# Stick-breaking running sums: one fp32 summand and two matmuls, against a high and a low fp32r part and four matmuls

## The chip, the cores and the metric

The kernel runs on one core of a Trainium2 chip. The metric is device time in microseconds of one execution. The kernel before takes 1051.0 us (median of 3 runs, 1050.75 to 1051.4).

## What is computed

The program is a two-layer encoder trunk on 256 tokens of width 1024: in each layer a SwiGLU block, a mixer, a second SwiGLU block and a gated embedding. The mixer of layer 0 has 8 forgetting-attention heads and 8 stick-breaking heads. The change touches the stick-breaking heads alone:

```python
def stick_breaking_attention(q, k, v):        # 8 heads, 256 tokens, head width 64
    z = einsum('bhqd,bhkd->bhqk', qi, k) * scale
    strict = kpos[None, :] < qpos[:, None]
    log_1m = where(strict, log_sigmoid(-z), 0.0)
    incl = cumsum(log_1m, axis=3, reverse=True)          # running sum over keys
    excl = concatenate([incl[..., 1:], 0], axis=-1)
    a = where(strict, exp(log_sigmoid(z) + excl), 0.0)
    return einsum('bhqk,bhkd->bhqd', a, v)
```

## The kernel before

Five engines run their own instruction lists and meet at semaphores. The order on each engine is written out by hand. Weights stream from HBM in chunks of 256 columns through a ring of four buffers (`raw`). ScalarE writes the high fp32r part of each half chunk (L585), VectorE the low part (L879), and TensorE multiplies three times (high by high, high by low, low by high). In the mixer such a product of 128 by 256 is L1292 to L1294, and for the value tiles L1485 to L1487.

The attention heads are laid as steps between these products. There are 16 heads in layer 0: steps 0 to 7 are forgetting attention, steps 8 to 15 the stick-breaking heads, which this text numbers 0 to 7. Up to head 2 one product tile of 24 matmuls stands between steps (`mixer_in`); from then on half tiles of 12 (`mixer_out`), two of them between an odd head's sums and those of the next even head.

Scores are kept with keys on the partitions, in a PSUM bank of 384 columns: keys 0 to 127 by all 256 queries, then keys 128 to 255 by queries 128 to 255. For a stick-breaking pair the steps are:

- TensorE, `stick_pair` (L1547, L1550, L1552): mask and scores of both heads.
- VectorE, `stick_abs` (L1123): absolute value into `probs`. For the odd head it waits (`buffers_free`) until the running sums of the odd head before it are done, since they read `probs`.
- ScalarE: exp (L773) and ln(1 + ...) (L775), in place.
- VectorE, `stick_sp` (L1129): max(score, 0) plus that logarithm, written over `probs`. This is the summand.
- TensorE, `middle` (L1589, L1590): a triangular matrix of minus ones times the summand is added onto the 384 columns of scores in PSUM, and a full matrix of minus ones times the last 128 columns onto the middle 128. Both are plain fp32.
- ScalarE (L767): exp of the bank into `probsT`. Then TensorE's `values_pair` (L1611, L1615), two steps later.

On VectorE an even step is: abs of the even head, low part of an older output (L1118), abs of the odd head, one L879, summand of the even head. An odd step is the summand of the odd head and one L879 if one is due. In `mixer_out` the residual addition L1158 stands between steps. On TensorE the sums of an odd head stand right behind `stick_pair` of the next pair, and those of an even head right behind a product tile (or two half tiles).

Of the kernel before, what the change touches and what calls it, by code (L numbers as in the profile page):

```python
# [5 lines left out]
ALU = mybir.AluOpType  # L6
ACT = mybir.ActivationFunctionType
AX_X = mybir.AxisListType.X
F32 = mybir.dt.float32
# [142 lines left out]
def trunk(nc, x, p, ln_ffn1, w_ffn1_gu, w_ffn1_down, ln_mix, w_in_even, b_forget, w_out_even, w_in_odd,  # L152
# [14 lines left out]
    with ExitStack() as ctx:  # L167
# [15 lines left out]
        with ExitStack() as region:  # L183
            osp = region.enter_context(nc.sbuf_tensor("osp", [P, KD, 2, SEQ], F32R))
            qT = region.enter_context(nc.sbuf_tensor("qT", [P, 8, SEQ], F32))
            kT = region.enter_context(nc.sbuf_tensor("kT", [P, 8, SEQ], F32))
            vN = region.enter_context(nc.sbuf_tensor("vN", [P, TOK, 2 * GROUP_W], F32))
        with ExitStack() as region:
            hankel = region.enter_context(nc.sbuf_tensor("hankel", [P, HEADS, 257], F32))
        with ExitStack() as region:  # L190
            xin = region.enter_context(nc.sbuf_tensor("xin", [P, TOK, D_MODEL], F32))
            gin = region.enter_context(nc.sbuf_tensor("gin", [P, P], F32))
            proj = region.enter_context(nc.sbuf_tensor("proj", [P, KD, SEQ], F32))
            yT = region.enter_context(nc.sbuf_tensor("yT", [P, KD, SEQ], F32))
            yN = region.enter_context(nc.sbuf_tensor("yN", [P, TOK, D_MODEL], F32))
            rel_sb = region.enter_context(nc.sbuf_tensor("rel_sb", [HEADS, 3 * P], F32))
        hff = sb("hff", [P, KF, 2, SEQ], F32R)


# [8 lines left out]
        bias = sb("bias", [P, HEADS, LOGITS], F32)  # L208
        probs = sb("probs", [P, 2, LOGITS + 2], F32)
        probsT = sb("probsT", [P, 4, LOGITS], F32)  # L210

        swa_scale = sb("swa_scale", [P, HEADS // 2], F32)
        mask_causal = sb("mask_causal", [P, LOGITS], F32)
# [19 lines left out]
        nhalf = sb("nhalf", [P, 2], F32)  # L233
        rcol = sb("rcol", [P, 2], F32)
        rtmp = sb("rtmp", [P, 2], F32)
        row_sq = sb("row_sq", [P, len(GATE_ROWS)], F32)
        rfin = sb("rfin", [P, TOK], F32)
        bf = sb("bf", [P, HEADS], F32)
        nsink = sb("nsink", [P, HEADS], F32)
        fl = sb("fl", [P, TOK, HEADS], F32)  # L240
        fa = sb("fa", [P, TOK, HEADS], F32)
        logf = sb("logf", [P, TOK, HEADS], F32)
        fcum = sb("fcum", [P, TOK, HEADS], F32)
        negmax = sb("negmax", [P, 2, 2], F32)
# [34 lines left out]
        k_swapped = sem("k_swapped")  # L279
        scores_done, logits_ready = sem("scores_done"), sem("logits_ready")  # L280
        exp_done, pt_done, pt_ready = sem("exp_done"), sem("pt_done"), sem("pt_ready")
        sb_abs, sb_e, sb_log, sb_sp, incl_done, sb_a = sem("sb_abs"), sem("sb_e"), sem("sb_log"), sem("sb_sp"), sem("incl_done"), sem("sb_a")
        norm_step, probs_ready, pv_done = sem("norm_step"), sem("probs_ready"), sem("pv_done")
        os_hi, os_lo = sem("os_hi"), sem("os_lo")
# [286 lines left out]
        def _(act):  # L571
# [124 lines left out]
            def mixer_in(ph, norm):  # L696
                if ph.layer == 1:
                    act.wait_ge(tile_done, state["T"])
                    src = bass.AP(rel_scratch, 0, [[1, P], [3 * P, HEADS], [1, 257]])
                    act.dma_start(hankel[:], src).then_inc(rel_back, 16)  # L700
                for n, (chunk, col, what, idx, scale) in enumerate(IN_TILES[ph.layer]):
                    next_tile()
                    if is_v(what):

                        if what == "v":
                            group, j, t = idx
                            start, w = GROUP_W * group + 256 * j, 256
                        else:
                            t, start, w = idx, GROUP_W, P
                        act.wait_ge(rcol_ready, norm + 1)  # L710
                        act.activation(vN[:, t, start:start + w], ps[:, in_bank(n), 0:w], ACT.Copy,
                                       scale=rcol[:, t:t + 1]).then_inc(v_ready, 1)
                    if not slots(ph.layer, n):
                        advance(in_units(ph, n))
                    if ph.layer == 1 and (what, idx) == ("vd", 0):

                        act.wait_ge(*written(1, n - 1))
                        act.dma_start(kT[0:HD, 5, :], kT[HD:P, 4, :]).then_inc(k_swapped, 16)
                        act.dma_start(kT[HD:P, 5, :], kT[0:HD, 4, :]).then_inc(k_swapped, 16)
                    if ph.layer == 1 and n == 3:  # L720
                        act.wait_ge(rel_back, 16)
                        for col, far in ((0, P), (P, 2 * P), (2 * P, P)):
                            act.activation(bias[:, :, col:col + P], hankel[:, :, far:far - P:-1], ACT.Copy,
                                           scale=-1.0).then_inc(chunk_bias, 1)
                    if ph.layer == 0 and n == FORGET_TILE + 1:

                        nc.scalar.preload_act_table_set("natural_log_exp_and_others")
                        act.wait_ge(f_step, 2)
                        act.activation(fa[:], fa[:], ACT.Exp, scale=-1.0).then_inc(f_act, 1)
                        act.wait_ge(f_act, 1)  # L730
                        act.activation(fa[:], fa[:], ACT.Ln, bias=1.0).then_inc(f_act, 1)
                    for i in slots(ph.layer, n):
                        attention_step(ph.layer, i)
                        advance(in_units(ph, n))
# [135 lines left out]
        def _(dve):  # L870
# [236 lines left out]
            def attention_step(layer, i, units):  # L1107


                first, n = 2 * HEADS * layer, 2 * HEADS  # L1110
                if layer == 1 and i == 0:
                    dve.wait_ge(chunk_mask, 2)
                g = first + i
                def low_of_values():
                    if 4 <= i and i % 2 == 0:
                        pair = (g - 4) // 2
                        dve.wait_ge(os_hi, pair + 1)
                        dve.tensor_tensor(osp[:, pair % KD, 1, :], ps[:, BANK_O[pair % 2], 0:SEQ], osp[:, pair % KD, 0, :].bitcast(F32),  # L1118
                                          ALU.subtract).then_inc(os_lo, 1)

                def stick_abs(e):
                    buffers_free(e)
                    dve.tensor_scalar(probs[:, e % 2, 0:LOGITS].bitcast(I32), ps[:, stick_bank(e), 0:LOGITS].bitcast(I32), NO_SIGN, None,  # L1123
                                      ALU.bitwise_and).then_inc(sb_abs, 1)

                def stick_sp(e):
                    row = probs[:, e % 2, 0:LOGITS]
                    dve.wait_ge(sb_log, stick_no[e] + 1)
                    dve.scalar_tensor_tensor(row, ps[:, stick_bank(e), 0:LOGITS], 0.0, row, ALU.max, ALU.add).then_inc(sb_sp, 1)  # L1129

                if i < n and is_sb[g] and i % 2 == 0:
                    stick_abs(g)
                    low_of_values()
                    stick_abs(g + 1)
                    advance(units)
                    stick_sp(g)
                elif i < n and is_sb[g]:
                    stick_sp(g)
                    advance(units)
                elif i < n and i % 2 == 0:  # L1140
                    logits(g)
                    low_of_values()
                    logits(g + 1)
                    advance(units)
                    normalise(g)
                elif i < n:
                    normalise(g)
                    advance(units)
                else:
                    low_of_values()  # L1150
                    advance(units)
# [126 lines left out]
        def _(pe):  # L1278
# [296 lines left out]
            def middle(g):  # L1575
                s = g % 2
                if not is_sb[g]:

                    pe.wait_ge(probs_ready, soft_no[g] + 1)
                    if soft_no[g]:  # L1580
                        pe.wait_ge(pt_ready, soft_no[g])
                    for b in range(3):
                        mm = pe.transpose(ps[:, BANK_PT, b * P:(b + 1) * P], probs[:, s, prob_block(b)], ident[:])  # L1583
                    mm.then_inc(pt_done, 1)
                else:

                    S, sp_ = ps[:, stick_bank(g)], probs[:, s]
                    pe.wait_ge(sb_sp, stick_no[g] + 1)
                    pe.matmul(S[:, 0:LOGITS], negtri[:], sp_[:, 0:LOGITS], start=False, stop=True, skip_group_check=True)  # L1589
                    pe.matmul(S[:, P:SEQ], negones[:], sp_[:, SEQ:LOGITS], start=False, stop=True,  # L1590
                              skip_group_check=True).then_inc(incl_done, 1)

            def values_pair(g):
# [210 lines left out]
```

## Time and profile before

| | |
|---|---|
| median of 3 runs | 1051.0 us |
| the profiled execution | 1051.11 us |
| its span | 1049.4 us |
| TensorE busy | 1034.7 us (99%) |
| VectorE busy | 757.6 us (72%) |
| ScalarE busy | 587.7 us (56%) |
| granted TensorE clock, mean | 0.997 of full speed |

The span runs from the first to the last instruction of the trace; 1.7 us of the execution lie around it. Busy times add up instructions. Matmul records overlap (a matmul of 256 columns is recorded as 0.28 us, and the next one begins 0.12 us after it), so for TensorE the distance between starts is what a matmul costs the stream.

### The profile page before, as it was taken

What the parts mean: (1) busy time and instruction counts of PE and PEld (TensorE: products, weight loads), DVE (VectorE), ACT (ScalarE), POOL (GpSimd) and SP (SyncE); (2) the same over time, 40 slices, a digit from 0 to 9 for tenths busy, and PEclk for the clock granted to TensorE, in tenths of its full rate; (3) what the DMA queues carried; (4) which work ended last, traced back from release to release, by engine and by line L of the source; (5) the groups of instructions that cost most, each with busy time, mean ns of one, the idle gap of its engine ahead of it and who ended that gap; (6) DMA issues with size and microseconds to landing.
All of it is one profiled execution on the core that took longest, in us unless ns stands there. A gap on an engine that the chain in (4) does not pass through costs nothing.

```text
span 1049.4 us, 18321 instructions
## 1 busy us (share of the span) xinstructions
PE 1034.7 (99%) x6624; PEld 926.4 (88%) x6624; DVE 757.6 (72%) x1352; ACT 587.7 (56%) x1002; POOL 52.0 (5%) x100
## 2 busy tenths in 40 slices
PE   9999999999999999999999999999999999999996
PEld 8888888999888888888998888889987888888896
DVE  5988765677558888666788778656766787786576
ACT  6666545445646566554566565445665665654463
POOL 1000001000002000000010000000000200000000
PEclk9999999999999999999999999999999999999998
DMA  9675457573324655456747664477733375645741
GB/s 317 212 232 165 143 159 214 174 240 113 121 91 156 220 185 186 138 163 202 231 129 239 197 197 133 144 207 237 242 97 111 118 240 197 197 134 145 205 158 41
DMA packets 225223, 184.46 MB, mean 176 GB/s; under 512 B 3640, under 2 KB 223504, under 8 KB 225168
## 3 DMA queue, kind: packets, MB, share of 16 engines
q1 hardware_dynamic: 222832, 180.94, 55.1%
q10 hardware_dynamic: 2336, 2.81, 0.9%
q8 instruction: 32, 0.52, 0.2%
q14 instruction: 23, 0.19, 0.1%
HBM read 182.54 MB, written 1.06 MB: 175 GB/s over the span
## 4 chain that ended last, share of the span: by engine, by line
PE 93%; DVE 3%; issue 1%; DMA 1%; ACT 1%; SPq 0%; DVEq 0%; ACTq 0%
PE ps L1370 42%; PE ps L1375 22%; PE ps L1292 4%; PE ps L1301 4%; PE ps L1293 4%; PE ps L1294 4%; PE ps L1485 2%; PE ps L1302 2%; PE ps L1486 2%; PE ps L1487 2%; DVE wsp L879 1%; PE ps L1570 1%; DMA raw<-in_w_ffn_gu_dram 1%; PE ps L1611 1%; PE ps L1583 1%
## 5 line engine op out<-in xcount | busy, mean ns | idle before, releaser
L879 DVE TENSOR_TENSOR wsp<-raw,wsp 128x1024 fp32r<-128x1024 f32 (+1 forms) x381 | 416.1, 1108 | 61.0 <-ACT wsp L585 60.2
L585 ACT ACTIVATE wsp<-raw 128x1024 fp32r<-128x1024 f32 (+1 forms) x381 | 354.5, 957 | 26.4 <-PE ps L1294 21.5
L1370 PE MATMUL ps<-xsA,wsp 128*128 128x512 f32 x960 | 229.0, 391 | 0.0
L1370 PEld LDWEIGHTS ps<-xsA,wsp 128*128 128x128 f32 x960 | 176.4, 188 | 34.3
L1370 PE MATMUL ps<-hff,wsp 128*128 128x512 f32 x616 | 145.0, 390 | 0.0
L1370 PEld LDWEIGHTS ps<-hff,wsp 128*128 128x128 f32 x616 | 113.8, 188 | 22.7
L1375 PEld LDWEIGHTS ps<-xsA,wsp 128*128 128x128 f32 x960 | 123.0, 191 | 4.5
L1375 PE MATMUL ps<-xsA,wsp 128*128 128x256 f32 x960 | 124.7, 283 | 0.0
L894 DVE TENSOR_TENSOR sq<-ps,sq 128x512 f32<-128x512 f32 x88 | 60.5, 687 | 87.6 <-ACT sq L601 87.2
L601 ACT ACTIVATE sq<-ps 128x512 f32<-128x512 f32 x88 | 51.9, 590 | 111.0 <-PE ps L1375 109.3
L647 ACT ACTIVATE xsA<-xT,gains 128x256 fp32r<-128x256 f32 x48 | 24.4, 507 | 135.2 <-DVE xT L1028 120.4
L1292 PE MATMUL ps<-xsA,wsp 128*128 128x256 f32 x296 | 85.7, 289 | 0.4 <-DVE wsp L879 0.4
L1293 PE MATMUL ps<-xsA,wsp 128*128 128x256 f32 x296 | 83.7, 283 | 0.0
L1294 PE MATMUL ps<-xsA,wsp 128*128 128x256 f32 x296 | 83.6, 283 | 0.0
L1370 PE MATMUL ps<-xsB,wsp 128*128 128x512 f32 x336 | 80.2, 391 | 0.0
L1375 PEld LDWEIGHTS ps<-hff,wsp 128*128 128x128 f32 x616 | 77.6, 191 | 2.2
L604 ACT ACTIVATE silu<-gate_n 128x256 f32<-128x256 f32 x88 | 37.0, 420 | 75.1 <-DVE gate_n L896 75.1
L1375 PE MATMUL ps<-hff,wsp 128*128 128x256 f32 x616 | 78.3, 283 | 0.0
L1370 PEld LDWEIGHTS ps<-xsB,wsp 128*128 128x128 f32 x336 | 61.7, 188 | 12.0
L896 DVE TENSOR_TENSOR gate_n<-sq,rstd 128x512 f32<-128x512 f32 x88 | 60.9, 692 | 3.0
L1292 PEld LDWEIGHTS ps<-xsA,wsp 128*128 128x128 f32 x296 | 56.7, 191 | 1.0 <-DVE wsp L879 0.6
L1293 PEld LDWEIGHTS ps<-xsA,wsp 128*128 128x128 f32 x296 | 56.7, 192 | 0.1
(204 smaller groups left out, 1452.6 us busy)
## 6 DMA issues: line engine op xcount, KB each, us to landing
raw<-in_w_ffn_gu_dram SPq DMA_DIRECT2D x87, 1024.0 KB, 5.1
raw<-in_w_ffn_down_dram SPq DMA_DIRECT2D x64, 704.0 KB, 4.7
raw<-in_w_in_even_dram SPq DMA_DIRECT2D x11, 1024.0 KB, 6.0
raw<-in_w_in_odd_dram SPq DMA_DIRECT2D x9, 1024.0 KB, 6.1
raw<-in_w_ple_gate_dram SPq DMA_DIRECT2D x8, 1024.0 KB, 6.2
raw<-in_w_out_even_dram SPq DMA_DIRECT2D x4, 1024.0 KB, 5.6
raw<-in_w_out_odd_dram SPq DMA_DIRECT2D x4, 1024.0 KB, 6.2
raw<-in_w_ple_proj_dram SPq DMA_DIRECT2D x2, 1024.0 KB, 5.1
```

Source lines behind the costliest of these rows:

```text
L585: act.activation(wsp[:, s, 0, half * n:(half + 1) * n], raw[:, s, half * n:(half + 1) * n], ACT.Copy).then_inc(hi, 1)
L601: act.activation(cross[:], ps[:, b:b + 3:2, SEQ:], ACT.Copy).then_inc(gu_cross, 1)
L604: act.activation(silu[:], gate_n[:, 0], ACT.Silu).then_inc(gu_silu, 1)
L879: dve.tensor_tensor(wsp[:, s, 1, sl], raw[:, s, sl], wsp[:, s, 0, sl].bitcast(F32), ALU.subtract).then_inc(lo, 1)
L894: dve.tensor_tensor(cross[:], ps[:, b:b + 3:2, 0:SEQ], cross[:], ALU.add).then_inc(gu_sum, 1)
L896: dve.tensor_tensor(gate_n[:], cross[:], rstd[:].unsqueeze(1).broadcast_to([P, 2, SEQ]), ALU.mult).then_inc(gu_norm, 1)
L1292: pe.matmul(out_, whi, moving[:, 0, :], start=first, stop=False)
L1293: pe.matmul(out_, whi, moving[:, 1, :], start=False, stop=False)
L1294: return pe.matmul(out_, wlo, moving[:, 0, :], start=False, stop=last)
L1301: pe.matmul(ps[:, bank, :], whi, moving.rearrange("p s t -> p (s t)"), start=first, stop=False)
L1370: pe.matmul(ps[:, bank, :], whi, moving.rearrange("p s t -> p (s t)"), start=first and i == 0, stop=False)
L1375: mm = pe.matmul(ps[:, bank, SEQ:], wlo, moving[:, 0, :], start=False, stop=last and i == len(blocks) - 1)
```

## The change

VectorE makes three arrays where it made one. The high part is the summand, written as fp32r (`sp_high`). The second operation takes max(score, 0) minus that high part into `rest`, which lies in `gate_n`. The third adds the logarithm and writes the low fp32r part (`sp_low`). Each of them waits for the one before by a semaphore. TensorE multiplies the triangular and the full matrix, now fp32r copies, with both parts. The triangular product of the high part waits for `sb_rest`, since it overwrites the scores that the second operation reads; that of the low part waits for `sb_sp`. ScalarE makes the fp32r copies of the two matrices once, at the first tile of the mixer of layer 0. Three small buffers move in memory (`fl`, `fa`, `row_sq`), and those behind `sp_low` lie 3 KB further on.

```diff
+            sp_high = region.enter_context(nc.sbuf_tensor("sp_high", [P, 2, LOGITS], F32R))
+            negtri_r = region.enter_context(nc.sbuf_tensor("negtri_r", [P, P], F32R))
+            negones_r = region.enter_context(nc.sbuf_tensor("negones_r", [P, P], F32R))
...
+        sp_low = sb("sp_low", [P, 2, LOGITS], F32R)
...
                     next_tile()
+                    if ph.layer == 0 and n == 0:
+                        act.wait_ge(consts, N_CONSTS)
+                        act.activation(negtri_r[:], negtri[:], ACT.Copy).then_inc(tri_ready, 1)
+                        act.activation(negones_r[:], negones[:], ACT.Copy).then_inc(tri_ready, 1)
...
+                rest = gate_n[:].rearrange("p a b -> p (a b)")[:, 0:LOGITS]
+
                 def stick_sp(e):
                     row = probs[:, e % 2, 0:LOGITS]
                     dve.wait_ge(sb_log, stick_no[e] + 1)
-                    dve.scalar_tensor_tensor(row, ps[:, stick_bank(e), 0:LOGITS], 0.0, row, ALU.max, ALU.add).then_inc(sb_sp, 1)
+                    high, low = sp_high[:, e % 2], sp_low[:, e % 2]
+                    S = ps[:, stick_bank(e), 0:LOGITS]
+                    dve.scalar_tensor_tensor(high, S, 0.0, row, ALU.max, ALU.add).then_inc(sb_high, 1)
+                    dve.wait_ge(sb_high, stick_no[e] + 1)
+                    dve.scalar_tensor_tensor(rest, S, 0.0, high.bitcast(F32), ALU.max, ALU.subtract).then_inc(sb_rest, 1)
+                    dve.wait_ge(sb_rest, stick_no[e] + 1)
+                    dve.tensor_tensor(low, rest, row, ALU.add).then_inc(sb_sp, 1)
...
-                    S, sp_ = ps[:, stick_bank(g)], probs[:, s]
+                    S, high, low = ps[:, stick_bank(g)], sp_high[:, s], sp_low[:, s]
+                    tri, ones = negtri_r[:], negones_r[:]
+                    if stick_no[g] == 0:
+                        pe.wait_ge(tri_ready, 2)
+                    pe.wait_ge(sb_rest, stick_no[g] + 1)
+                    pe.matmul(S[:, 0:LOGITS], tri, high, start=False, stop=True, skip_group_check=True)
                     pe.wait_ge(sb_sp, stick_no[g] + 1)
-                    pe.matmul(S[:, 0:LOGITS], negtri[:], sp_[:, 0:LOGITS], start=False, stop=True, skip_group_check=True)
-                    pe.matmul(S[:, P:SEQ], negones[:], sp_[:, SEQ:LOGITS], start=False, stop=True,
+                    pe.matmul(S[:, 0:LOGITS], tri, low, start=False, stop=True, skip_group_check=True)
+                    pe.matmul(S[:, P:SEQ], ones, high[:, SEQ:LOGITS], start=False, stop=True, skip_group_check=True)
+                    pe.matmul(S[:, P:SEQ], ones, low[:, SEQ:LOGITS], start=False, stop=True,
                               skip_group_check=True).then_inc(incl_done, 1)
```

VectorE around the pair of heads 2 and 3 (L1123 is the absolute value, L879 a half chunk of weights, L1118 an older output), before:

```order
L1123 TENSOR_SCALAR probs<-ps 128x384 [waits incl_done,scores_done]
L879 TENSOR_TENSOR wsp<-raw,wsp 128x1024 [waits hi]
L1129 SCALAR_TENSOR_TENSOR probs<-ps,probs 128x384 [waits sb_log]
L1129 SCALAR_TENSOR_TENSOR probs<-ps,probs 128x384 [waits sb_log,tile_done]
L879 TENSOR_TENSOR wsp<-raw,wsp 128x1024 [waits hi]
```

The same place of VectorE in the changed kernel:

```order
L1133 TENSOR_SCALAR probs<-ps 128x384 [waits incl_done,scores_done]
L889 TENSOR_TENSOR wsp<-raw,wsp 128x1024 [waits hi]
L1143 SCALAR_TENSOR_TENSOR sp_high<-ps,probs 128x384 [waits sb_log]
L1145 SCALAR_TENSOR_TENSOR gate_n<-ps,sp_high 128x384 [waits sb_high]
L1147 TENSOR_TENSOR sp_low<-gate_n,probs 128x384 [waits sb_rest]
L1143 SCALAR_TENSOR_TENSOR sp_high<-ps,probs 128x384 [waits sb_log,tile_done]
L1145 SCALAR_TENSOR_TENSOR gate_n<-ps,sp_high 128x384 [waits sb_high]
L1147 TENSOR_TENSOR sp_low<-gate_n,probs 128x384 [waits sb_rest]
L889 TENSOR_TENSOR wsp<-raw,wsp 128x1024 [waits hi]
```

Nothing changes place; two operations are put in behind each of the two summands, ahead of the next half chunk of weights.

TensorE at the sums of head 1, between the scores of the next pair and a value tile, before:

```order
L1552 MATMUL ps<-qT,kT 128x128 x2
L1589 MATMUL ps<-probs,negtri 128x384 [waits sb_sp]
L1590 MATMUL ps<-probs,negones 128x128
L1485 MATMUL ps<-wsp,xsA 128x256 [waits v_ready,lo]
```

The same place of TensorE in the changed kernel:

```order
L1570 MATMUL ps<-qT,kT 128x128 x2
L1610 MATMUL ps<-sp_high,negtri_r 128x384 [waits sb_rest]
L1612 MATMUL ps<-sp_low,negtri_r 128x384 [waits sb_sp]
L1613 MATMUL ps<-sp_high,negones_r 128x128
L1614 MATMUL ps<-sp_low,negones_r 128x128
L1503 MATMUL ps<-wsp,xsA 128x256 [waits v_ready,lo]
```

The two products become four in the same place, with one wait more, and everything behind them on TensorE keeps its order.

## Rows read from the trace of the kernel before

**Rows 1.** The page: busy times, and shares of the chain that ended last.
```profile
PE 1034.7 (99%) x6624; PEld 926.4 (88%) x6624; DVE 757.6 (72%) x1352; ACT 587.7 (56%) x1002; POOL 52.0 (5%) x100
...
PE 93%; DVE 3%; issue 1%; DMA 1%; ACT 1%; SPq 0%; DVEq 0%; ACTq 0%
```
**Rows 2.** Busy time by stretch (window, length, PE, PEld, DVE, ACT, POOL, clock, DMA).
```profile
271.80:302.40 30.60, 30.60 (x231) 25.18 (x230) 18.59 (x31) 19.18 (x38) 0.00 (x0) 1.00 0.41 133
```
**Rows 3.** PE timeline at head 0: start us, us, engine, line.
```profile
276.13 0.28 PE L1487 MATMUL ps<-wsp,xsA 128*128 128x256 f32 x1
276.25 0.82 PE L1589 MATMUL ps<-probs,negtri 128*128 128x384 f32 x2
276.91 0.38 PE L1590 MATMUL ps<-probs,negones 128*128 128x128 f32 x2
277.05 0.36 PE L1485 MATMUL ps<-wsp,xsA 128*128 128x256 f32 x1
277.25 0.28 PE L1486 MATMUL ps<-wsp,xsA 128*128 128x256 f32 x1
```
**Rows 4.** PE timeline, fp32r steps of 512 and 256 columns, then of 128.
```profile
321.22 0.40 PE L1301 MATMUL ps<-xsA,wsp 128*128 128x512 f32 x1
321.46 0.28 PE L1302 MATMUL ps<-xsA,wsp 128*128 128x256 f32 x1
321.58 0.40 PE L1301 MATMUL ps<-xsA,wsp 128*128 128x512 f32 x1
...
765.96 0.27 PE L1485 MATMUL ps<-wsp,xsA 128*128 128x128 f32 x1
766.07 0.28 PE L1486 MATMUL ps<-wsp,xsA 128*128 128x128 f32 x1
```
**Rows 5.** DVE operation L1129, grouped by shape over the stretch 255 to 312 us.
```profile
L1129 DVE SCALAR_TENSOR_TENSOR probs<-ps,probs 128x384 f32<-128x384 f32 x8 | 4.4, 554 | 1.9 <-PE ps L1487 1.0 <-ACT probs L775 0.9
```
**Rows 6.** DVE timeline, an operation and one that waits for its result.
```profile
267.97 0.15 DVE L1101 RECIPROCAL rinv<-rowsum 128x2 f32<-128x2 f32 x1
268.16 0.55 DVE L1104 TENSOR_SCALAR probs<-probs,rinv 128x128 f32<-128x128 f32 x2
```
**Rows 7.** Timeline of DVE and PE where a product waits for DVE.
```profile
322.72 1.21 DVE L945 SCALAR_TENSOR_TENSOR xsA<-xT,gains,xsA 128x256 fp32r<-128x256 f32 x2
...
323.99 0.50 PE L1301 MATMUL ps<-xsA,wsp 128*128 128x512 f32 x1
...
324.33 0.28 PE L1302 MATMUL ps<-xsA,wsp 128*128 128x256 f32 x1
```
**Rows 8.** DVE timeline over the heads (an excerpt), with idle time before.
```profile
275.55 0.55 DVE L1129 SCALAR_TENSOR_TENSOR probs<-ps,probs 128x384 f32<-128x384 f32 x1
...
283.31 0.56 DVE L1123 TENSOR_SCALAR probs<-ps 128x384 int32<-128x384 int32 x1 [0.20 <-PE ps L1590]
283.79 1.22 DVE L879 TENSOR_TENSOR wsp<-raw,wsp 128x1024 fp32r<-128x1024 f32 x1
284.92 0.55 DVE L1129 SCALAR_TENSOR_TENSOR probs<-ps,probs 128x384 f32<-128x384 f32 x1
286.11 0.56 DVE L1129 SCALAR_TENSOR_TENSOR probs<-ps,probs 128x384 f32<-128x384 f32 x1 [0.64 <-PE ps L1487]
...
290.09 0.56 DVE L1123 TENSOR_SCALAR probs<-ps 128x384 int32<-128x384 int32 x1 [0.25 <-PE ps L1590]
...
298.29 0.56 DVE L1129 SCALAR_TENSOR_TENSOR probs<-ps,probs 128x384 f32<-128x384 f32 x1 [0.86 <-ACT probs L775]
298.76 0.41 DVE L1158 TENSOR_TENSOR xT<-ps,xT 128x256 f32<-128x256 f32 x1
```
**Rows 9.** PE timeline: L1589 of heads 2 and 4 to 7.
```profile
285.91 0.81 PE L1589 MATMUL ps<-probs,negtri 128*128 128x384 f32 x2
...
292.69 0.81 PE L1589 MATMUL ps<-probs,negtri 128*128 128x384 f32 x2
...
295.62 0.91 PE L1589 MATMUL ps<-probs,negtri 128*128 128x384 f32 x2
...
299.46 0.81 PE L1589 MATMUL ps<-probs,negtri 128*128 128x384 f32 x2
...
301.22 0.91 PE L1589 MATMUL ps<-probs,negtri 128*128 128x384 f32 x2
```
**Rows 10.** ACT timeline at the start of the mixer of layer 0.
```profile
197.50 4.90 ACT L585 ACTIVATE wsp<-raw 128x1056 fp32r<-128x1056 f32 x5 [1.14 <-PE ps L1294]
203.74 1.06 ACT L585 ACTIVATE wsp<-raw 128x1024 fp32r<-128x1024 f32 x1 [1.34 <-PE ps L1294]
```

More of the change, by code:

```diff
@@ L187, in trunk @@
             vN = region.enter_context(nc.sbuf_tensor("vN", [P, TOK, 2 * GROUP_W], F32))
+            sp_high = region.enter_context(nc.sbuf_tensor("sp_high", [P, 2, LOGITS], F32R))
+            negtri_r = region.enter_context(nc.sbuf_tensor("negtri_r", [P, P], F32R))
+            negones_r = region.enter_context(nc.sbuf_tensor("negones_r", [P, P], F32R))
+        with ExitStack() as region:
+            fl = region.enter_context(nc.sbuf_tensor("fl", [P, TOK, HEADS], F32))
+            fa = region.enter_context(nc.sbuf_tensor("fa", [P, TOK, HEADS], F32))
         with ExitStack() as region:
@@ L196, in trunk @@
             rel_sb = region.enter_context(nc.sbuf_tensor("rel_sb", [HEADS, 3 * P], F32))
+            row_sq = region.enter_context(nc.sbuf_tensor("row_sq", [P, len(GATE_ROWS)], F32))
         hff = sb("hff", [P, KF, 2, SEQ], F32R)
@@ L235, in trunk @@
         rtmp = sb("rtmp", [P, 2], F32)
-        row_sq = sb("row_sq", [P, len(GATE_ROWS)], F32)
         rfin = sb("rfin", [P, TOK], F32)
@@ L239, in trunk @@
         nsink = sb("nsink", [P, HEADS], F32)
-        fl = sb("fl", [P, TOK, HEADS], F32)
-        fa = sb("fa", [P, TOK, HEADS], F32)
         logf = sb("logf", [P, TOK, HEADS], F32)
@@ L281, in trunk @@
         exp_done, pt_done, pt_ready = sem("exp_done"), sem("pt_done"), sem("pt_ready")
+        tri_ready, sb_high, sb_rest = sem("tri_ready"), sem("sb_high"), sem("sb_rest")
         sb_abs, sb_e, sb_log, sb_sp, incl_done, sb_a = sem("sb_abs"), sem("sb_e"), sem("sb_log"), sem("sb_sp"), sem("incl_done"), sem("sb_a")
```

## The prediction, made before the changed kernel was run

> **What bounds the kernel now.** I read the page first: TensorE is busy 99% of the span and makes 93% of the chain that ended last [rows 1]. So what changes the end is either the time that TensorE spends on an instruction, or a new gap in its stream. The busy times of the stretch of the stick-breaking heads come next: from 271.8 to 302.4 us TensorE is busy in all of the 30.60 us, at a granted clock of 1.00, while VectorE has 18.59 us of work [rows 2]. That looks like 12 us of room on VectorE. The room that counts is a different one: how long before TensorE arrives a summand is ready. At head 0 the summand starts at 275.55 and takes 0.55, so it ends at 276.10 [rows 8], and TensorE's L1589 starts at 276.25 [rows 3]: 0.15 us early. At head 2 it ends at 284.92 + 0.55 = 285.47 [rows 8] against 285.91 [rows 9]: 0.44 us. Head 3's starts at 286.11 [rows 8] and is wanted only behind the scores of the next pair, some 2 us later. So even heads have almost no room, and odd heads have room at first.
>
> **TensorE, part by part.** A step is the distance between starts. Plain fp32: L1589 to L1590 is 276.91 - 276.25 = 0.66. From L1589 to the second matmul behind the sums is 277.25 - 276.25 = 1.00 [rows 3]; one ordinary step of 0.12 off, the sums cost 0.88 us a head, some 0.08 of it a slower first step of the following tile.
> fp32r: 512 columns step by 321.46 - 321.22 = 0.24, 256 by 321.58 - 321.46 = 0.12, 128 by 766.07 - 765.96 = 0.11 [rows 4]. 384 columns are not shown; the rows on both sides bound them at 0.12 and 0.24, and I take 0.175, near the middle. The new sums are 2 x 0.175 + 2 x 0.11 = 0.57. The two small products gain nothing: at 128 columns an fp32r step costs 0.11, half of the 0.22 that 0.88 - 0.66 leaves for L1590 and its change of mode, and there are two. So TensorE gives back 0.88 - 0.57 = 0.31 us a head, 2.5 us over 8 heads, if nothing waits. By the bounds of the 384 columns it is 0.42 or 0.18 a head.
>
> **VectorE, part by part.** The summand takes 554 ns, eight times [rows 5]. The second operation has the same form (one operand in PSUM, one in SBUF), and I give it and the third 0.55 too. Operations that do not wait for each other overlap a little: abs at 283.31 to L879 at 283.79 is 0.48 for an operation of 0.56, and L879 at 283.79 to the summand at 284.92 is 1.13 for 1.22 [rows 8]. One that waits for the result of the last starts after its end: the reciprocal starts at 267.97, lasts 0.15, and its reader starts at 268.16, so 0.04 after the end [rows 6]. So three operations in a chain last 3 x 0.55 + 2 x 0.035 = 1.72 us, and VectorE gets 1.17 us more of work a head, 9.4 us over 8 heads. Bounds: 0.48 a step, the overlapped one, makes the chain 1.51; the scalar-pointer form L945, two in 1.21 us for 256 columns [rows 7], with 0.13 for 128 columns more, makes it 0.73 x 3 = 2.2. I take 1.72, from the row of the same form.
>
> The Trainium skill, in "VectorE: DVE Perf Modes", section "The DRAIN you can't avoid", says that eight copies cost the same with a semaphore behind each as with one behind the last. The rows above disagree in part (0.48 against 0.59 a step), and what follows if the page is right is a rival below. The same page advises to keep the number of operations small, whatever the semaphores: that speaks against this change.
>
> **What a broken wait adds.** L945 ends at 322.72 + 1.21 = 323.93 and the product that needs it starts at 323.99; its own step is 324.33 - 323.99 = 0.34, against 0.24 unhindered [rows 7, 4]. So from the end of the VectorE operation to full stream TensorE loses 0.06 + 0.10 = 0.16. Where TensorE stands waiting for the low part, the sums end 0.16 + 0.175 + 0.22 = 0.555 after the low part is written; the high product is done in the meantime.
>
> **The sum, head by head** (lateness of TensorE at the end of the sums, against before).
> Head 0: low part written 275.55 + 1.72 = 277.27, sums end 277.82. Before: 276.25 + 0.88 = 277.13. Late by 0.69.
> Head 1: the summand has time (VectorE done by 279), and the sums are 0.31 shorter: 0.38.
> Head 2: abs of head 3 waits for the sums of head 1, so it moves from 283.31 to 283.69. Then 0.48 and 1.13 bring the summand to 285.30, the low part to 287.02, the sums to 287.58, against 285.91 + 0.88 = 286.79: 0.79.
> Head 3: 0.48. Its half chunk L879 now stands behind two chains and ends about 289.7, when the next abs is due anyway.
> Head 4: the same loop, from abs at 290.09 + 0.48: low part 293.90, sums 294.46, against 292.69 + 0.88 = 293.57: 0.89.
> Head 5: from here VectorE itself is the late one. Behind head 4's low part stand L1158 (0.34), L879 (1.13) and head 5's chain, so its low part is written at 293.82 + 0.34 + 1.13 + 1.72 = 297.01, when TensorE has been there since 295.62 + 0.89 = 296.51. Sums end 297.57, before 296.59: 0.98.
> Head 6: its summand waited for ScalarE at 298.29 [rows 8], and ScalarE was behind the exp of head 5, so it moves with head 5's sums to 299.27. Low part 300.99, sums 301.55, against 299.46 + 0.88 = 300.34: 1.21.
> Head 7: L1158 (0.34) and a chain behind head 6's: 300.91 + 0.34 + 1.72 = 302.97, sums 303.53. Before, 301.22 + 0.97 = 302.19: 1.34.
> (All of the starts of before are in rows 3, 8 and 9; odd heads cost 0.97, since the 64-row scores ahead of them slow the first step.) Behind head 7 TensorE has products to the end, so the 1.3 us stay.
>
> **Priced at nothing.** The two copies on ScalarE, at most 0.36 us each, start at 197.50, ahead of five half chunks that end at 202.40. Then ScalarE waits 1.34 us to 203.74 [rows 10]; 0.72 fits. Without that cover they would cost up to 0.7. L879 being up to 3 us later delays the load of the chunk four further on, by that much out of a turn of the ring of more than 20 us; no engine waits for such a load in this stretch. Buffers lie elsewhere; nothing in the trace prices that, and I leave 0.3 us of the range for it.
>
> So the profiled execution would go from 1051.1 to 1052.4, and the median, which is 0.1 lower, from 1051.0 to 1052.3.
>
> **Rivals.**
> A. Waiting for a result costs VectorE nothing, as the page says. Chain 1.51 in the same walk: lateness 0.48, 0.17, 0.38, 0.07, 0.28, then 0.17, 0.18 and 0.11 at heads 5 to 7. Time 1051.1. For it: the overlap at 283.31. Against: the gap at 268.16 [rows 8, 6].
> B. The added work on VectorE is covered and TensorE's gain comes through: 8 x 0.31 = 2.5 us less, 1048.5. For it: VectorE is idle for 12 of 30.6 us. Against: the 0.15 and 0.44 us of room at heads 0 and 2, which 1.17 more does not fit in.
> C. The slower side. The fp32r product with 384 moving columns runs at the rate of plain fp32, 0.33 for each part (half of 0.66). Then there is no gain at all on TensorE, and the walk gives 0.84, 0.84, 1.41, 1.41, 1.98, 2.08, 2.46, 2.6: 1053.6, 0.25% slower. It decides from 0.29 a product on. For it: at 128 columns fp32r has no better rate than plain. Against: 512 and 256 columns stand on a line through 0.24 and 0.12.
>
> **How the numbers follow.** A difference within 0.2%, 2.1 us, can't be told from none here: 1048.9 and 1053.1 are the borders. Forecast (chain of 1.6 to 1.85 us, 384 columns at 0.16 to 0.2): 0.66, with 1051.6 to 1053.2 as its own range; about a tenth of it lies over the border, where the chain costs more (each 0.1 us of chain is worth about 0.6 us in the end, for six of the heads hand their lateness on; the 2.2 us bound would make it 1055). A: 0.16. C: 0.10. B: 0.05. Something unseen: 0.03. Faster 0.05, the same 0.78, slower 0.17. The range runs from just below A to just below C, 1050.9 to 1053.4.
>
> **What would show it.** Right: at heads 0, 2 and 4 a gap on TensorE ahead of the low product with VectorE as its releaser; three VectorE operations 0.58 to 0.6 apart; 384 columns stepping by 0.16 to 0.19; odd heads 1 and 3 without a gap, heads 5 to 7 with one; the stretch 271.8 to 302.4 longer by about 1.3 and the rest of the span equal. Wrong: steps of 0.48 (A), no gaps (B), steps of 0.3 or more at 384 columns (C), or a difference that arises outside this stretch.

## The result, and the profile after

The changed kernel takes 1052.75 us (median of 20 runs, 1051.86 to 1054.04), the kernel before 1051.14 us (20 runs, 1050.55 to 1053.07). The ratio is 1.0014, with a 95% interval from 1.0007 to 1.002: slower by 1.6 us, less than 0.2%. The prediction was 1052.3 us, with "the same within 0.2%" as the likeliest outcome.

The page of the changed kernel, busy times and shares of the chain, against [rows 1]:

```profile
PE 1034.7 (99%) x6624; PEld 926.8 (88%) x6624; DVE 765.9 (73%) x1368; ACT 588.2 (56%) x1004; POOL 51.7 (5%) x100
...
PE 92%; DVE 5%; issue 2%; ACT 1%; DVEq 0%; POOL 0%; ACTq 0%; POOLq 0%
```

VectorE has 16 instructions and 8.3 us of busy time more, and its share of the chain goes from 3% to 5%. TensorE's busy time is equal to a tenth of a microsecond, which tells nothing, since its records overlap. The stretch of the heads says more, by the busy times of the stretch (columns as in [rows 2]):

```profile
271.80:302.40 30.60, 29.40 (x222) 24.29 (x221) 25.74 (x46) 18.76 (x37) 0.00 (x0) 1.00 0.38 127
```

TensorE is busy for 29.40 us of 30.60, not for all of it, and VectorE for 25.74 in place of 18.59. The clock is at full speed (2.4 GHz) there in both. Where the gaps are, the waits of the whole trace tell (who waited for whom, us in total, times, longest):

```profile
PEld ps L1612 <- DVE sp_low L1147: 2.4, 6, 0.4
...
PEld ps L1610 <- DVE gate_n L1145: 0.7, 3, 0.2
```

Both are new, and both wait for the chain on VectorE: for the low part (L1147) and for the second operation (L1145). The six waits for the low part stand at heads 0, 2, 4, 5, 6 and 7; heads 1 and 3 have none. TensorE at head 0, as a timeline, to be read against [rows 3]:

```profile
276.32 0.41 PE L1610 MATMUL ps<-sp_high,negtri_r 128*128 128x384 f32 x1 [0.43 <-DVE gate_n L1145]
276.82 0.45 PE L1612 MATMUL ps<-sp_low,negtri_r 128*128 128x384 f32 x1
277.11 0.22 PE L1613 MATMUL ps<-sp_high,negones_r 128*128 128x128 f32 x1
277.17 0.27 PE L1614 MATMUL ps<-sp_low,negones_r 128*128 128x128 f32 x1
277.28 0.34 PE L1503 MATMUL ps<-wsp,xsA 128*128 128x256 f32 x1
277.45 0.28 PE L1504 MATMUL ps<-wsp,xsA 128*128 128x256 f32 x1
```

TensorE stands idle for 0.43 us ahead of the high product, which starts 276.32 + 0.53 - 276.25 = 0.60 us later than L1589 did (the 0.53 is the shift explained under "Lateness by head"). The low one starts 0.50 us behind it; then the stream runs on. Head 1, where the chain was done long before:

```profile
282.28 0.44 PE L1610 MATMUL ps<-sp_high,negtri_r 128*128 128x384 f32 x1
282.56 0.34 PE L1612 MATMUL ps<-sp_low,negtri_r 128*128 128x384 f32 x1
282.74 0.22 PE L1613 MATMUL ps<-sp_high,negones_r 128*128 128x128 f32 x1
282.80 0.27 PE L1614 MATMUL ps<-sp_low,negones_r 128*128 128x128 f32 x1
```

An fp32r step of 384 columns behind another is 282.74 - 282.56 = 0.18 us; 0.175 was taken. A first one, behind the 64-row scores or behind a wait, is 0.28 or 0.29. The scores slowed the first step of head 1 before as well, to 282.82 - 282.07 = 0.75 against 0.66 at head 0:

```profile
282.07 0.91 PE L1589 MATMUL ps<-probs,negtri 128*128 128x384 f32 x2
282.82 0.38 PE L1590 MATMUL ps<-probs,negones 128*128 128x128 f32 x2
```

VectorE's timeline over head 0's chain, and from head 4's residual addition to the start of head 6's chain, against [rows 8]:

```profile
275.03 0.55 DVE L1143 SCALAR_TENSOR_TENSOR sp_high<-ps,probs 128x384 fp32r<-128x384 f32 x1
275.62 0.56 DVE L1145 SCALAR_TENSOR_TENSOR gate_n<-ps,sp_high 128x384 f32<-128x384 f32 x1
276.21 0.56 DVE L1147 TENSOR_TENSOR sp_low<-gate_n,probs 128x384 fp32r<-128x384 f32 x1
276.69 0.55 DVE L1143 SCALAR_TENSOR_TENSOR sp_high<-ps,probs 128x384 fp32r<-128x384 f32 x1
...
293.33 0.42 DVE L1176 TENSOR_TENSOR xT<-ps,xT 128x256 f32<-128x256 f32 x1
293.66 1.22 DVE L889 TENSOR_TENSOR wsp<-raw,wsp 128x1024 fp32r<-128x1024 f32 x1
294.79 0.55 DVE L1143 SCALAR_TENSOR_TENSOR sp_high<-ps,probs 128x384 fp32r<-128x384 f32 x1
295.38 0.56 DVE L1145 SCALAR_TENSOR_TENSOR gate_n<-ps,sp_high 128x384 f32<-128x384 f32 x1
295.97 0.56 DVE L1147 TENSOR_TENSOR sp_low<-gate_n,probs 128x384 fp32r<-128x384 f32 x1
296.45 0.42 DVE L1176 TENSOR_TENSOR xT<-ps,xT 128x256 f32<-128x256 f32 x1
296.78 0.55 DVE L1133 TENSOR_SCALAR probs<-ps 128x384 int32<-128x384 int32 x1
...
298.73 0.56 DVE L1143 SCALAR_TENSOR_TENSOR sp_high<-ps,probs 128x384 fp32r<-128x384 f32 x1 [0.60 <-ACT probs L785]
```

Operations that wait for the result of the last stand 0.59 apart; the next one, which does not wait, comes after 0.48. From 282.91, behind the abs of head 2, to the abs of head 7 at 297.58 no row has an idle time: VectorE works without a pause. Then it waits 0.60 us for ScalarE (L785) ahead of head 6's chain, which starts at 298.73.

**Lateness by head.** The profiled changed kernel is earlier at the first scores of the mixer (239.00 us against 239.53, a difference that arises at the start of the program: the first product with weights already starts at 8.81 against 9.36). So each trace is shifted to make its first scores coincide, and then the second matmul behind each head's sums is compared with before. All tables below are made in this way. Over heads 0 to 7:

| | 0 | 1 | 2 | 3 | 4 | 5 | 6 | 7 |
|---|---|---|---|---|---|---|---|---|
| predicted | 0.69 | 0.38 | 0.79 | 0.48 | 0.89 | 0.98 | 1.21 | 1.34 |
| measured | 0.73 | 0.44 | 0.84 | 0.54 | 0.90 | 1.03 | 1.19 | 1.36 |

For head 0 that is 277.45 - 277.25 + 0.53 = 0.73, by the timeline above and [rows 3]. The 1.36 us stay and hardly anything is added in the 450 us behind them: the first scores of the mixer of layer 1 come at 749.94 after and 749.06 before, so 749.94 - 239.00 = 510.94 us against 509.53 behind those of layer 0, 1.41 more. At the end of the span it is 1.45.

### The profile page after: what moved, and what is told of

It reads as the page before. It is cut to its first block, busy times and chain, and to the rows that moved or that the text cites. A ratio compares the mean times of both kernels' runs of the same rounds, so it can differ in the third digit from the quotient of the medians.

```text
span 1050.3 us, 18341 instructions
## 1 busy us (share of the span) xinstructions
PE 1034.7 (99%) x6624; PEld 926.8 (88%) x6624; DVE 765.9 (73%) x1368; ACT 588.2 (56%) x1004; POOL 51.7 (5%) x100
## 4 chain that ended last, share of the span: by engine, by line
PE 92%; DVE 5%; issue 2%; ACT 1%; DVEq 0%; POOL 0%; ACTq 0%; POOLq 0%
PE ps L1388 42%; PE ps L1393 22%; PE ps L1319 4%; PE ps L1310 4%; PE ps L1311 4%; PE ps L1312 4%; PE ps L1320 2%; PE ps L1503 2%; PE ps L1505 2%; PE ps L1504 2%; DVE wsp L889 2%; PE ps L1588 1%; PE ps L1601 1%; DVE probs L1104 1%; PE ps L1635 1%
## 5 line engine op out<-in xcount | busy, mean ns | idle before, releaser
L889 DVE TENSOR_TENSOR wsp<-raw,wsp 128x1024 fp32r<-128x1024 f32 (+1 forms) x381 | 416.3, 1109 | 59.9 <-ACT wsp L591 59.0
```

The lines of the kernel that those rows point to most:

```text
L889: dve.tensor_tensor(wsp[:, s, 1, sl], raw[:, s, sl], wsp[:, s, 0, sl].bitcast(F32), ALU.subtract).then_inc(lo, 1)
```

## Experiments

Theory 1: the loss is the chain of three VectorE operations, which even heads have no room for, and VectorE's total work from head 4 on. Theory 2: each head pays a like price on TensorE, for one wait more, cold steps and the change of mode. Medians come from 6 to 11 runs each; the kernel before ran beside them, 1051.1 to 1051.2 us.

**The four matmuls without their price on VectorE.**

```diff
-                    dve.scalar_tensor_tensor(high, S, 0.0, row, ALU.max, ALU.add).then_inc(sb_high, 1)
...
-                    dve.tensor_tensor(low, rest, row, ALU.add).then_inc(sb_sp, 1)
+                    dve.scalar_tensor_tensor(high, S, 0.0, row, ALU.max, ALU.add).then_inc(sb_sp, 1)
...
-                    pe.matmul(S[:, 0:LOGITS], tri, low, start=False, stop=True, skip_group_check=True)
+                    pe.matmul(S[:, 0:LOGITS], tri, high, start=False, stop=True, skip_group_check=True)
```

> The four fp32r matmuls without their price on VectorE: one operation writes the high part, and both pairs of matmuls read it (the low part is left out, the high one is added twice). Theory 1 (the time goes into the chain of three VectorE operations, which even heads have no room for): with the chain gone TensorE's gain comes through, 0.31 to 0.34 us a head, 2.5 to 2.7 us in all: about 1048.5 us, no wait of TensorE for a summand, and the lateness at head 7 is about -2.6 us. Theory 2 (each head pays the same small price on TensorE, for cold weight loads, a wait more and the change of mode, whatever VectorE does): no faster than the kernel before, 1051 to 1052.

Measured: 1049.61 us, ratio 0.9979 (0.997 to 0.9988). Lateness -0.23, -0.53, -0.86, -1.04, -1.37, -1.68, -2.01, -2.31: every head gives back 0.18 to 0.33, 0.29 on average, where 0.31 to 0.34 was expected. So TensorE's gain is real, and theory 2 falls. The median gained only 1.6 us of these 2.3, and the profiled execution lost 1.35 again in layer 1, as told under the clock below.

**Odd heads alone, and even heads alone.**

```diff
+        def split_head(k):
+            return k % 2 == 1          # k % 2 == 0 in the other kernel
...
+                    if not split_head(stick_no[e]):
+                        dve.scalar_tensor_tensor(row, S, 0.0, row, ALU.max, ALU.add).then_inc(sb_sp, 1)
+                        return
```

The same condition stands on TensorE, with the two plain matmuls of before.

> Odd heads in the new form, even heads in the old one. Nothing is left out. Theory 1: odd heads have the time for the chain (about 2 us of room at head 3), so each gives back 0.34 us, and VectorE has four operations less to hold up heads 5 to 7: lateness -0.3, -0.3, -0.7, -0.7, -1.0, -1.0, -1.4 over heads 1 to 7, in all -1.3 us, about 1049.8. Theory 2: half of what the full change costs, +0.7 us, about 1051.8.

> Even heads in the new form, odd heads in the old one. Nothing is left out. Theory 1: every even head waits for its chain and nothing is given back between them: lateness about 0.7 after head 0, 1.1 after head 2, 1.5 after head 4, 1.7 after head 6: +1.7 us, about 1052.8, more than the full change although half of its work is gone. Theory 2: +0.7 us, about 1051.8.

| lateness | 0 | 1 | 2 | 3 | 4 | 5 | 6 | 7 | median us | ratio |
|---|---|---|---|---|---|---|---|---|---|---|
| odd only | 0.02 | -0.27 | -0.25 | -0.55 | -0.54 | -0.32 | -0.33 | -0.62 | 1051.11 | 0.9999 (0.999 to 1.0008) |
| even only | 0.72 | 0.72 | 1.11 | 1.10 | 1.49 | 1.49 | 1.70 | 1.70 | 1052.76 | 1.0013 (1.0004 to 1.0022) |

The even heads do what theory 1 says, to 0.02 us: they lose 0.72 at head 0 and 0.2 to 0.4 at each later one, more in all than the full change loses. Odd heads 1, 3 and 7 give back 0.29 or 0.30 each, where 0.34 was expected. Head 5 does not: it loses 0.2. I had given it the same room as head 3. The median of the odd heads alone, expected at 1049.8, can't be told from the kernel before. In the trace (its lines have other numbers: L892 is the half chunk, L1150 to L1154 the chain, L1627 the low product) the half chunk comes late, for it waits for ScalarE, and TensorE then waits for head 5's low part:

```profile
292.71 1.23 DVE L892 TENSOR_TENSOR wsp<-raw,wsp 128x1024 fp32r<-128x1024 f32 x1 [0.85 <-ACT wsp L594]
293.86 0.55 DVE L1150 SCALAR_TENSOR_TENSOR sp_high<-ps,probs 128x384 fp32r<-128x384 f32 x1
...
295.64 0.44 PE L1627 MATMUL ps<-sp_low,negtri_r 128*128 128x384 f32 x1 [0.15 <-DVE sp_low L1154]
```

**VectorE's part alone.**

```diff
-                    pe.wait_ge(sb_rest, stick_no[g] + 1)
-                    pe.matmul(S[:, 0:LOGITS], tri, high, start=False, stop=True, skip_group_check=True)
+                    S, sp_ = ps[:, stick_bank(g)], sp_high[:, s].bitcast(F32)
                     pe.wait_ge(sb_sp, stick_no[g] + 1)
...
+                    pe.matmul(S[:, 0:LOGITS], negtri[:], sp_[:, 0:LOGITS], start=False, stop=True, skip_group_check=True)
+                    pe.matmul(S[:, P:SEQ], negones[:], sp_[:, SEQ:LOGITS], start=False, stop=True,
```

> VectorE as in the change (three operations a head), TensorE as before: two plain fp32 matmuls, on the high part, once the third operation is done (the low part is computed and left out). Theory 1: the same chain, but after it 0.88 us of sums and no gain at odd heads, and since abs of the next odd head waits for them, lateness runs up: 1.0, 1.0, 1.9, 1.9, 2.8, 2.9, 3.6, 3.8: about 1054.9 us. Theory 2: the price sits on TensorE's new products, and these are gone: 1051 to 1052.

Measured: 1055.0 us, ratio 1.0035 (1.0023 to 1.0047), lateness 1.17, 1.16, 2.07, 2.07, 2.98, 3.05, 3.78, 3.89. The three operations cost 3.9 us at the end, of which the faster products give back 2.5. Here the expected 3.8 was met as well.

**Head 5: the half chunk ahead of its chain.** In the odd-only trace the order at head 5 is residual addition, half chunk, then the chain (in the numbers of the kernel before: L1158, L879). Two kernels move that one half chunk, called by `advance` behind the first residual addition, to behind head 5's summand: odd heads alone, and the full change.

```diff
                     dve.tensor_tensor(xT[:, m], ps[:, out_bank(ph.layer, m), 0:SEQ], xT[:, m], ALU.add).then_inc(half_resid, 1)
-                    advance(2 * (ph.c0 + RING))
+                    if ph.layer == 1 or m:
+                        advance(2 * (ph.c0 + RING))
```

> The new form at odd heads alone, and in layer 0 the last half chunk of weights on VectorE, which stands between the residual addition and the summand of head 5, goes behind that summand. Nothing is left out. In the odd-heads run TensorE was 0.54 us early after head 4 and only 0.32 early after head 5. Theory 1 (at head 5 the chain starts late, because that half chunk first waits for ScalarE): with it out of the way heads 5 and 7 give back their 0.3 each; lateness -0.85 after head 5, -1.15 after head 7, about 1049.9 us. Theory 2 (an odd head has no room in mixer_out whatever stands ahead, since two half tiles leave VectorE too little time): still about -0.3 after head 5 and -0.6 at the end.

> The full change with the same half chunk moved behind the summand of head 5. Nothing is left out. Theory 1: head 5 no longer waits and is shorter than before by 0.34, so lateness after it is 0.56 in place of 1.03; but the half chunk is then ahead of abs of head 6, so heads 6 and 7 get back only a part: about 0.95 and 1.1, 1052.3 us. Theory 2: no change against the full change, 1.03 after head 5 and 1.36 at the end.

| lateness | 0 | 1 | 2 | 3 | 4 | 5 | 6 | 7 | median us | ratio |
|---|---|---|---|---|---|---|---|---|---|---|
| odd only, moved | 0.03 | -0.27 | -0.25 | -0.56 | -0.54 | -0.84 | -0.83 | -1.12 | 1051.03 | 0.9994 (0.9985 to 1.0003) |
| full change, moved | 0.76 | 0.46 | 0.86 | 0.56 | 0.92 | 0.62 | 0.97 | 1.13 | 1052.14 | 1.001 (1.0001 to 1.0019) |

Both go as theory 1 has it: the half chunk was what head 5 stood behind. In the full change half of the gain is lost again at head 6, since the half chunk is now ahead of its abs.

**The chain ahead of the half chunk at even heads.**

```diff
                     stick_abs(g + 1)
+                    stick_sp(g)
                     advance(units)
-                    stick_sp(g)
```

> The full change, with the chain of an even head ahead of the half chunk of weights on VectorE in every even step. Nothing is left out. Theory 1 (what counts at even heads is when the low part is written): the chain can start once ScalarE has its logarithm, 0.47 us earlier at head 0 and 0.2 us earlier at head 2, but the half chunk then stands ahead of the odd head's chain and of the next abs, and VectorE is late by itself from head 3 on: lateness about 0.27, -0.07, 0.15, -0.1, 0.7 over heads 0 to 4 and 1.0 to 1.2 at the end, about 1052.1 us. If only the place of the half chunk mattered and not VectorE's total work, the gain would stay: 0.5 at the end, 1051.6.

Measured: 1053.2 us, ratio 1.0018 (1.0009 to 1.0027), lateness 0.24, -0.05, 0.12, -0.10, 0.63, 1.89, 2.04, 2.21. Up to head 4 all values came within 0.07 of the expected ones. Then head 5 lost 1.3 us, where 0.3 to 0.5 was expected from there to the end. VectorE's timeline:

```profile
291.72 0.56 DVE L1143 SCALAR_TENSOR_TENSOR sp_high<-ps,probs 128x384 fp32r<-128x384 f32 x1 [0.36 <-ACT probs L785]
292.31 0.56 DVE L1145 SCALAR_TENSOR_TENSOR gate_n<-ps,sp_high 128x384 f32<-128x384 f32 x1
292.91 0.56 DVE L1147 TENSOR_TENSOR sp_low<-gate_n,probs 128x384 fp32r<-128x384 f32 x1
293.38 1.22 DVE L889 TENSOR_TENSOR wsp<-raw,wsp 128x1024 fp32r<-128x1024 f32 x1
294.52 0.42 DVE L1176 TENSOR_TENSOR xT<-ps,xT 128x256 f32<-128x256 f32 x1
294.85 1.22 DVE L889 TENSOR_TENSOR wsp<-raw,wsp 128x1024 fp32r<-128x1024 f32 x1
295.99 0.55 DVE L1143 SCALAR_TENSOR_TENSOR sp_high<-ps,probs 128x384 fp32r<-128x384 f32 x1
```

Two half chunks (L889) now stand between head 4's chain and head 5's, and VectorE idled 0.36 us ahead of head 4's chain. It had already waited 0.81 us for ScalarE ahead of head 2's chain (at 284.44), where the full change has no pause. Counted from the first scores of the mixer, head 5's chain starts at 295.99 - 239.33 = 56.66 us, against 294.79 - 239.00 = 55.79 in the full change: 0.87 later, and head 5's lateness is 1.89 against 1.03. On an engine that is full, to put the urgent work first and wait for its input costs such waits.

**A clock that falls in some executions.** The odd-only kernel with the move is 1.1 us early at head 7, yet its median is equal to before. Its 11 times fall into 1049.5 to 1049.9 (four) and 1050.9 to 1051.6 (seven), with nothing between. The four-free kernel's profiled execution shows what differs, in busy times by microsecond (the granted clock stands before the last two columns):

```profile
790.00:791.00 1.00, 0.00 (x0) 0.00 (x0) 0.96 (x4) 1.00 (x3) 0.80 (x2) 1.00 0.00 0
791.00:792.00 1.00, 0.65 (x5) 0.49 (x7) 0.96 (x6) 0.46 (x2) 0.00 (x0) 0.99 0.35 23
792.00:793.00 1.00, 1.00 (x8) 0.50 (x6) 1.00 (x2) 1.00 (x2) 0.00 (x0) 0.50 0.90 269
793.00:794.00 1.00, 1.00 (x10) 0.82 (x8) 1.00 (x3) 0.70 (x2) 0.00 (x0) 0.50 1.08 385
794.00:795.00 1.00, 1.00 (x5) 0.35 (x4) 0.75 (x2) 0.00 (x0) 0.00 (x0) 0.50 1.09 370
795.00:796.00 1.00, 1.00 (x8) 1.00 (x8) 1.00 (x6) 0.36 (x1) 0.00 (x0) 0.80 0.21 48
```

In layer 1, at step 10 of the mixer, TensorE idles 1.75 us, up to 791.35, for VectorE (L1104 in the kernel before, behind a half chunk). Within a microsecond behind that wait the granted clock falls to 0.50 (1.2 GHz) and stays there for 3.4 us, from 792.0 to 795.4. Nine of the profiled executions have the wait of 1.75 us, and three of these the fall (four-free, even-only, odd-only moved). From the first scores of layer 1 to the end of the span these three take 301.50 to 301.68 us, the other six 300.30 to 300.45: the fall costs some 1.2 us. To see whether the fall follows the wait, the wait was shortened, in the kernel before:

```diff
                     logits(g + 1)
-                    advance(units)
-                    normalise(g)
+                    if layer == 1 and i == 10:
+                        normalise(g)
+                        advance(units)
+                    else:
+                        advance(units)
+                        normalise(g)
```

> The kernel before, with one thing moved in layer 1: at step 10 VectorE scales the probabilities (L1101, L1104) ahead of the half chunk of weights L879, not behind it. It is no part of the change. TensorE waits 1.75 us there for L1104 in every trace so far, and in some executions its granted clock fell to half for about 3.5 us right behind that wait, which cost 1.2 us more. Theory a (the fall follows that wait): TensorE waits about 0.8 us, the times are 0.96 us lower, and the executions that are 1.2 us longer than the rest become rare, so the spread shrinks too: median about 1050.0, few over 1051. Theory b (the fall has nothing to do with it): median 1050.2, with the same share of executions 1.2 us above the rest.

Measured: 1051.11 us, ratio 0.9998 (0.9989 to 1.0007). All 11 times lie between 1050.65 and 1051.43; of the 33 runs of the kernel before beside them 12 were longer than that. The mean granted clock of each run says it more plainly: 25 of all 84 runs of the kernel before in these comparisons had 0.996 or less, and of the 40 runs of the four kernels with the shortened wait (this one and the three that follow) none had. (A fall can hide in 0.997 as well: the profiled execution of the moved odd-only kernel has it.) So the long executions vanished, but the 0.94 us that TensorE won at step 10 was lost at step 12:

```profile
793.17 0.55 PE L1587 MATMUL ps<-ident,probs 128*128 128x128 f32 x3 [0.81 <-DVE probs L1104]
...
799.91 0.55 PE L1587 MATMUL ps<-ident,probs 128*128 128x128 f32 x3 [1.20 <-DVE probs L1104]
```

**Two moves together.** Odd heads alone, the half chunk behind head 5, and the scaling first at step 10 of layer 1.

> The new form at odd heads alone, with both moves (the half chunk behind the summand of head 5 in layer 0, the scaling ahead of its half chunk at step 10 in layer 1). Nothing is left out. The two lie 480 us apart on a TensorE that is busy in between, so their gains should add: 1.15 and 0.96 us, and less of the 1.2 us of clock: about 1048.8 us, against 1051.2 before. If the gain in layer 0 were lost again in layer 1 (TensorE only arriving earlier at that wait), it would be 1050.

Measured: 1049.98 us, ratio 0.9987 (0.9978 to 0.9996), all 11 times within 1049.59 and 1050.21. The gain of layer 0 came through in full; that of the wait was lost at step 12, so it is 1050.0 and not 1048.8.

**Step 12 of layer 1.** The scaling goes first there too, and the half chunk behind the first residual addition goes to that step. First on the kernel before, then on the odd-only kernel with all moves.

```diff
-                    advance(units)
-                    normalise(g)
+                    if layer == 1 and i in (10, 12):
+                        normalise(g)
+                        advance(units)
...
-                    advance(2 * (ph.c0 + RING))
+                    if m:                      # in the kernel before: ph.layer == 0 or m
+                        advance(2 * (ph.c0 + RING))
```

> The kernel before with two things moved in layer 1: the scaling of the probabilities ahead of the half chunk at steps 10 and 12, and the half chunk behind the first residual addition taken to step 12. With the first move alone TensorE's wait of 1.75 us became 0.81, and a new one of 1.20 us arose at the scaling of step 12, behind a half chunk. Theory a (that half chunk is the whole cause of the new wait): both waits shrink, 0.94 + 1.0 us earlier in all, about 1049.2 us, none of the executions 1.2 us above the rest. Theory b (step 12 is bound by ScalarE or by the scores): the wait stays near 1.2, 1051.1 us as in the run before.

> The new form at odd heads alone, the half chunk behind the summand of head 5 in layer 0, and both moves in layer 1. Nothing is left out. If the gains add: 1.12 us in layer 0 and about 1.9 in layer 1, about 1048.1 us against 1051.1 before and 1050.0 for the two moves. If step 12 of layer 1 is bound otherwise: 1050.0.

Measured: 1050.06 us, ratio 0.9986 (0.9977 to 0.9995), and 1048.98 us, ratio 0.9973 (0.9961 to 0.9984). TensorE's timeline of the first has one wait left between 789 and 812 us:

```profile
792.86 0.55 PE L1588 MATMUL ps<-ident,probs 128*128 128x128 f32 x3 [0.82 <-DVE probs L1104]
```

The wait of 1.20 is gone with that half chunk out of the way, so it was the cause. The gain in layer 1 is 1.0 us, not the 1.9 expected: I had counted the 0.94 of step 10 and the new wait as two gains, but removing that new wait only brings the first gain back. The last kernel, with -1.13 at head 7, is the fastest of all and beats the kernel before by 2.2 us; it leaves nothing of the computation out. About half of that is the change at odd heads with its moved half chunk (1048.98 against 1050.06), the other half the moves in layer 1, which are no part of the change.

## Why the prediction was right

**What bounds.** Right. TensorE's stream sets the time of the kernel, and the room of 0.15 and 0.44 us at even heads, not VectorE's 12 idle microseconds, decided. The four-free and VectorE-alone runs show both sides of the sum: 2.3 us given back, where the sum had 2.5, and 3.9 us lost, where the same walk without TensorE's gain (worked out ahead of that run) had 3.8.

**TensorE's steps.** 384 columns at 0.18 us: right. The small products were mis-sized: I had 2 x 0.11, and the rows above show 277.17 - 277.11 = 0.06 and 277.28 - 277.17 = 0.11. So 128 fp32r columns can stream in 0.06 us; 0.11 is what a product costs in the run of such products in [rows 4], and what the last one costs here, ahead of a product with other weights. Against that, the next tile's first step still costs 277.45 - 277.28 = 0.17 in place of 0.12, which I had counted in the old sums and not in the new ones. The two errors of 0.05 cancel, which is luck: an odd head gives back 0.29, predicted 0.31. The slow first step behind the 64-row scores costs 0.1 before and after, so it takes no part in the difference.

**VectorE's steps.** Each operation 0.55 to 0.56, 0.59 from start to start, a chain of 1.74 (275.03 to 276.77): predicted 1.72. The 9.4 us of added work counted the pauses in the chain as work; the page of the changed kernel has 8.3 more. The Trainium skill states in "VectorE: DVE Perf Modes", section "The DRAIN you can't avoid", that eight copies with a semaphore behind each cost no more than with one behind the last. No run here compares an operation with and without a semaphore. What costs here is the wait for the result: 0.59, against 0.48 behind L1147, which sets a semaphore too, but one that the next operation of VectorE does not wait for. Rival A, which took such a wait to be free, would have ended at +0.1 us.

**The broken wait.** From the end of the low part (276.77) to its product 0.05, that product 0.29, then 0.17: 0.51 in all. The sum's yardstick includes the 0.05 of the next tile's slower first step, so it is 0.56 by that, predicted 0.555.

**Heads 5 to 7.** Right in the full change, that VectorE itself is the late one (no idle time up to the abs of head 7), and that head 6's chain waits for ScalarE (298.73 + 0.53 = 299.26, predicted 299.27). That it depends on one half chunk was in the sum, but I did not draw from it that head 5 has no room even when even heads are left alone, and so missed the odd-only run by 0.8 us at the end (-0.62, expected -1.4).

**Priced at nothing.** Right for the two copies on ScalarE: they take 0.31 and 0.29 us, and from the first product with weights to the first scores of the mixer it is 230.19 us after (239.00 - 8.81) and 230.17 before (239.53 - 9.36). The moved buffers were not tested alone; the four-free kernel has them too, and gives back nearly all of what was expected.

**Rivals.** B (all of the work covered) fell with TensorE's waits, C (384 columns at the plain rate) with the 0.18.

**What was missed.** The medians differ by 1.6 us and the traces by 1.4, and the interval of the ratio, 0.7 to 2.1 us, does not tell these apart. A part may be the fall of the clock, which the prediction did not know of. Of the 20 times after, 8 have a mean granted clock of 0.996 or less; the other 12 have a median of 1052.3. Of the 84 runs of the kernel before beside the experiments, the 59 with a clock of 0.997 or more have a median of 1051.0, 1.3 below. That the changed kernel meets the fall more often is not shown: 8 of 20 against 25 of 84 is too near. Why the clock falls in some executions and not in others behind the same wait is open.

## What to carry to other kernels

An engine that is idle 40% of a stretch may have no room at all where it counts: compare, for each wait of the bound engine, when the input is written and when it is wanted. Where there is room at every second place only, make the change at those places. Here the whole change is 1.6 us slower, and the odd heads alone, with one half chunk moved out of head 5's way, are 1.1 us faster (1049.98 against 1051.11, both with the scaling first at step 10). Without that move their gain was not clear of the noise. And a gain at one wait may only move to the next one, so look at the next wait behind the same engine before counting it.

## What the runs showed of the hardware that was not expected

- Shifted to the same start, traces repeat closely where nothing was changed: from the first scores of layer 0 to those of layer 1 it is 509.53 us in the kernel before and 509.57 and 509.53 in the two variants of it that differ only behind that. So a single trace tells a tenth of a microsecond, which medians of 11 runs don't.
- Behind an idle time of 1.75 us, in a stretch where TensorE was otherwise busy, the granted clock fell to half (1.2 GHz) for 3.4 us in three of nine profiled executions and stayed at 2.4 GHz in six, and the fall costs 1.2 us. With the idle time cut to 0.81 us none of 40 runs of four kernels had a mean granted clock under 0.997, and 25 of 84 runs of the kernel before had (two of these four kernels had a wait of 1.20 us as well).
- An fp32r product of 128 columns steps by 0.06 us ahead of another with the same matrix (L1613), and by 0.11 ahead of one with other weights (L1614) or in a run of such products ([rows 4]).
